# Taking two-head value matmuls apart, and moving two decay steps behind the compressed normalisation, in a two-block fp32 model kernel

## What is computed

```python
for l in range(DEPTH):                       # 2 layers
    proj = rms_norm(x, attn_norm[l]) @ w_in[l]
    ret_o = retention(rope(r_q), rope(r_k), r_v, r_g)      # 6 heads of 64
    nsa_o = nsa(n_q, n_kv, n_g, ...)                       # 6 heads of 64, 2 key/value groups
    gm_o = spatial_gating(gm_z, gm_ws[l], gm_b[l])
    x = x + concatenate([ret_o, nsa_o, gm_o]) @ w_out[l]
    gate, up = split(rms_norm(x, ffn_norm[l]) @ w_gate_up[l])
    x = x + (silu(gate) * up) @ w_down[l]
# nsa, for each head: out = g0 * o_c + g1 * o_s + g2 * o_w
#   o_c: softmax over 15 compressed keys;  o_s, o_w: softmax(q @ k.T + bias) @ v, selected and window branch
# retention, for each head: scores = (q @ k.T) * decay;  o = scores @ v, normalised and gated
```

## Time and profile before

| what | value |
|---|---|
| median of 3 runs | 2002.25 us (2001.49 to 2005.66) |
| the profiled execution: time | 2002.25 us |
| the profiled execution: span of the core | 2000.4 us |
| granted TensorE clock, mean | 0.98 |
| TensorE busy (matmul) | 1882.9 us, 94% |
| VectorE busy | 740.8 us, 37% |
| ScalarE busy | 240.3 us, 12% |
| GpSimd busy | 226.1 us, 11% |

### The profile page before, as it was taken

How to read it: one execution, slowest core, us unless ns; L and a number is a source line. 1 busy time by engine, 2 the same in 40 slices (tenths; PEclk the granted TensorE clock), 3 DMA queues, 4 the chain that set the end, 5 groups by cost and what they waited for, 6 DMA issues and landing times.

```text
span 2000.4 us, 22267 instructions
## 1 busy us (share of the span) xinstructions
PE 1882.9 (94%) x8302; PEld 919.2 (46%) x8302; DVE 740.8 (37%) x1560; ACT 240.3 (12%) x482; POOL 226.1 (11%) x400
## 2 busy tenths in 40 slices
PE   8999999999999999869799999999999999999995
PEld 4466777645577766635433333323332332332331
DVE  3562111155547761794522223222222322322224
ACT  1410000023110000211211101100110110110010
POOL 0200000001018857141000000000000000000000
PEclk9999999999999999979699999999999999999998
DMA  7143433343278845021699999999999999999993
GB/s 300 63 169 133 164 130 126 128 173 121 96 294 319 345 169 218 1 84 53 269 429 429 430 427 429 429 430 426 429 429 430 426 429 429 430 426 429 429 430 164
DMA packets 42766, 583.33 MB, mean 292 GB/s; under 512 B 4726, under 2 KB 5750, under 8 KB 6684
## 3 DMA queue, kind: packets, MB, share of 16 engines
q1 hardware_dynamic: 42236, 581.29, 70.1%
q10 hardware_dynamic: 480, 1.37, 0.2%
HBM read 581.58 MB, written 1.06 MB: 291 GB/s over the span
## 4 chain that ended last, share of the span: by engine, by line
PE 55%; DMA 34%; DVE 9%; ACT 1%; issue 1%; SPq 0%; ACTq 0%; DVEq 0%
DMA ring<-in_exp_w 33%; PE PS L1676 15%; PE PS L1957 10%; PE PS L1404 8%; PE PS L1695 7%; PE PS L1988 3%; PE PS L1581 3%; DVE ring L1107 1%; PE PS L1861 1%; PE PS L1943 1%; PE PS L1918 1%; DMA par<-in_layer_params 1%; PE PS L1451 0%; PE PS L1965 0%; PE PS L1442 0%
## 5 line engine op out<-in xcount | busy, mean ns | idle before, releaser
L1957 PE MATMUL PS<-ring,tb 128*64 128x512 f32 x2176 | 487.2, 598 | 32.6 <-DMA ring<-in_exp_w 31.9
L1957 PEld LDWEIGHTS PS<-ring,tb 128*64 128x64 f32 x2176 | 149.1, 137 | 366.1 <-issue 289.2
L1676 PE MATMUL PS<-hT,ring 128*128 128x256 f32 x1376 | 300.6, 379 | 0.0
L1676 PEld LDWEIGHTS PS<-hT,ring 128*128 128x128 f32 x1376 | 261.1, 190 | 43.0 <-issue 8.6
L1988 PE MATMUL PS<-ring,tb 128*64 128x512 f32 x1088 | 241.0, 595 | 11.5 <-ACT tb L652 11.5
L1404 PE MATMUL PS<-ring,hT 128*128 128x512 f32 (+2 forms) x448 | 187.0, 559 | 2.2 <-ACT hT L407 2.1
L1307 DVE TENSOR_TENSOR hT<-hT,PS 128x512 f32<-128x512 f32 x140 | 96.2, 687 | 233.8 <-PE PS L1943 231.4
L1320 DVE TENSOR_SCALAR tT<-PS 128x512 f32<-128x512 f32 x34 | 23.5, 692 | 425.0 <-PE PS L1965 425.0
L1695 PE MATMUL PS<-ring,tT 128*128 128x512 f32 x352 | 154.7, 593 | 0.0
L1988 PEld LDWEIGHTS PS<-ring,tb 128*64 128x64 f32 x1088 | 77.7, 137 | 152.8 <-issue 152.8
L1035 DVE TENSOR_TENSOR tT<-PS,tT 128x512 f32<-128x512 f32 x22 | 15.2, 692 | 269.6 <-PE PS L1676 269.6
(11 more groups left out here) (426 smaller groups left out, 1612.9 us busy)
## 6 DMA issues: line engine op xcount, KB each, us to landing
ring<-in_exp_w SPq DMA_DIRECT2D x204, 2048.0 KB, 22.8
ring<-in_w_gate_up SPq DMA_DIRECT2D x22, 2048.0 KB, 8.6
ring<-in_ada_w SPq DMA_DIRECT2D x12, 2048.0 KB, 9.2
ring<-in_w_in_part SPq DMA_DIRECT2D x10, 2048.0 KB, 10.2
ring<-in_w_down SPq DMA_DIRECT2D x10, 2048.0 KB, 7.2
ring<-in_w_out SPq DMA_DIRECT2D x6, 2048.0 KB, 8.5
ring<-in_w_in SPq DMA_DIRECT2D x4, 2048.0 KB, 8.2
ring<-in_w_in_part SPq DMA_DIRECT2D x2, 1608.0 KB, 11.6
```

What stands on the lines that cost most here:

```text
L1676: ins = pe.matmul(PS[:, 4 + 2 * (i % 2) + part, 256 * f:256 * f + 256], wt[:, k, 256 * part + 128 * f:256 * part + 128 * f + 128], hT[:, k ...
L1957: ins = pe.matmul(PS[64 * h:64 * h + 64, b, :], xg[:, o:o + 64], ring[:, s, w:w + 512], start=k == 0, stop=False, skip_group_check=True)
```

## The change

Two edits. In the TensorE list, `values` takes one head instead of a pair and is called twice in a step: for head 2p-2 between the second `project(2)` and `turn(2p-1)`, and for head 2p-1 where the pair stood. In the VectorE list, `decayed(2)` and `decayed(3)` move from ahead of the wait for the exponential (`s_c11`) to behind the last step of the compressed softmax.

```diff
@@ VectorE
                 link.to(v.tensor_tensor(pc2, pc2, st[:, 36:48].unsqueeze(2).broadcast_to([P, 12, NCMP]), ALU.subtract), g.s_c10, l + 1)
-                decayed(2)
-                decayed(3)
                 v.wait_ge(g.s_c11, l + 1)
                 link(v.tensor_reduce(st[:, 48:60], pc2, AX_X, ALU.add))
...
                 link.to(v.tensor_tensor(pc2, pc2, st[:, 48:60].unsqueeze(2).broadcast_to([P, 12, NCMP]), ALU.mult), g.s_c12, l + 1)
+                decayed(2)
+                decayed(3)
                 projected(6)
                 decayed(4)
                 decayed(5)
@@ TensorE
-                def values(p):
-                    pe.wait_ge(g.s_pt, l * 12 + 2 * p + 2)
-                    at, vs = [], []
-                    for c in (2 * p, 2 * p + 1):
-                        br, h = c // NH, c % NH
-                        o = (SV, WV)[br] + 64 * (h // 3)
-                        vs.append([proj[:, t, o:o + 64] for t in range(TT)])
-                        at.append((slice(64 * (h % 2), 64 * (h % 2) + 64), 6 + h // 4, 256 * (h // 2 % 2)))
-                    first = p // 3 == 0 and p % 3 in (0, 2)
-                    for i, (rows, bank, o) in enumerate(at):
-                        pe.matmul(PS[rows, bank, o:o + 256], vs[i][0], PT[i][:, 0:256], start=first, stop=False, skip_group_check=True)
-                    for i, (rows, bank, o) in enumerate(at):
-                        pe.matmul(PS[rows, bank, o + 128:o + 256], vs[i][1], PT[i][:, 256:384], start=False, stop=False,
-                                  skip_group_check=True).then_inc(g.s_pv, 1)
+                def values(c):
+                    br, h = c // NH, c % NH
+                    pe.wait_ge(g.s_pt, l * 12 + c + 1)
+                    o = (SV, WV)[br] + 64 * (h // 3)
+                    rows, bank, at = slice(64 * (h % 2), 64 * (h % 2) + 64), 6 + h // 4, 256 * (h // 2 % 2)
+                    pe.matmul(PS[rows, bank, at:at + 256], proj[:, 0, o:o + 64], PT[c % 2][:, 0:256], start=br == 0 and h in (0, 1, 4, 5), stop=False,
+                              skip_group_check=True)
+                    pe.matmul(PS[rows, bank, at + 128:at + 256], proj[:, 1, o:o + 64], PT[c % 2][:, 256:384], start=False, stop=False,
+                              skip_group_check=True).then_inc(g.s_pv, 1)
...
                     project(2)
                     if p >= 1:
+                        values(2 * p - 2)
                         turn(2 * p - 1)
...
                     project(2)
                     if p >= 1:
-                        values(p - 1)
+                        values(2 * p - 1)
```

## The result

The changed kernel takes 2019.41 us (median of 7 runs, 2013.19 to 2020.14), the kernel before, run beside it, 2005.66 us (7 runs, 2001.49 to 2007.66). The ratio is 1.007, with a 95% interval of 1.0059 to 1.0082: slower by 12 to 16 us, 0.7%. Forecast were 12.3 us more, but from a base of 2002.25, and a range up to 2019.0; the time lies 0.4 us outside it. The executions of the kernel before fall into two groups by their mean granted clock: of 64 that ran beside the experiments, 26 took 2000.7 to 2002.6 us at 0.979 or 0.980 and 38 took 2004.7 to 2009.6 us at 0.974 to 0.978, and the profiled one, 2002.25 us at 0.98, belongs to the first.

What follows compares the result with a forecast made beforehand. TensorE's work list in written order was taken to set the time, with delays passed on whole. Value groups 9.6 plus decays 2.7 gave 12.3 us, so 2002.25 + 12.3 = 2014.5 us; range 2009 to 2019 for 8 in 10.

Steps and rivals of the forecast that it cites:

- the sum's base: Whole kernel: the profiled 2002.25 us, also the median of the runs shown, to which 12.3 us were added.
- The decays: Compressed softmax and ret_scores(2): later decays lose 2.12 us, win back 0.78; +1.34 us per layer, +2.7 in all.
- The value groups: Attention steps: each added narrow group pays streaming and edges, 0.78 us in ten steps, 0.89 in two; +9.6 us.
- Rival A: Value groups: edges cost nothing more, 7.5 + 2.7 = 10.2 us, so 2012.4 us; chance 0.80 together with the forecast.
- rival B: Value groups: halves only seem to run together, a single head costs half; 2006.8 us; chance 0.07.
- C: Value groups: a single head can't hide weight loads behind a partner, 9.6 us more; 2024 us; chance 0.05.
- common starts: Paired value matmuls: records start two together, read as both halves running beside each other, a group taking 0.80 us.
- Rival D: Second transposition in the steps: heads fit wholly into a TensorE standstill, decays free; 1995.8 us; chance 0.03.
- The row of the weight loader's idle time: Before the transpositions: 6.5 us idle in 8 cases, put down to VectorE; the most a standstill could hide.
- Rival E: Expert loop: the delay vanishes because expert loads run on and TensorE had slack; 2002.3 us; chance 0.05.
- the second transposition's copy: ScalarE's copy in each step, late by 0.8 us; cover about 1 us, beyond which it is on the path.
- the gating: VectorE work behind the moved decays, wanted by later transposes; ends near 137.8 us, with 1.8 us of cover.

Runs made afterwards that it cites:

- e3: Kernel before, with both heads' value matmuls at the step's end, one head after the other instead of interleaved; 2001.78 us, ratio 0.999.
- e7: Kernel before, with decayed(2) and decayed(3) moved behind projected(6); 2009.35 us, ratio 1.0035.
- e10: Changed kernel with decayed(2) put back in its old place, decayed(3) still moved; 2013.97 us, ratio 1.005.
- e12: Repeat of the kernel before with only decayed(3) moved behind the compressed softmax; one execution, 2007.03 us.
- e9: Kernel of e2 plus 14 unread identity transposes on TensorE ahead of ret_scores(2); 2008.24 us, ratio 1.0021 to the kernel before.
- e11: The changed kernel once more, unaltered; one execution, 2018.74 us.
- e2: Kernel before with only decayed(2) and decayed(3) moved behind the compressed softmax, value matmuls still in pairs; 2013.40 us, ratio 1.0033.
- e1: Changed kernel with both decays back in their old place, so only the value matmuls are taken apart; 2015.69 us, ratio 1.0046.
- e4: Changed kernel with compressed_turn() and a project(4) ahead of ret_scores(2) in TensorE's list; 2014.60 us, ratio 1.0039 to the kernel before.
- e8: Kernel of e1 with the even head's 128-column matmul moved to the step's end, its 256-column one still early; 2008.37 us, ratio 1.0027.

## Why the prediction was wrong, point by point

**The step that failed is the sum's base.** The prediction said: "The profiled execution took 2002.25 us (span 2000.4), which is also the median of the runs". This equality holds for the three runs that were shown. Beside the changed kernel, seven runs gave 2005.66. The traces show where the difference lies. In the last column of the tables the same untouched code takes 1471.1 to 1477.1 us in 14 profiled executions, without order by kernel: the kernel before has 1471.92, e3, whose two layers are equal to it within 0.06 us, 1476.43. Two places carry it in these two. One is the stretch from the first L1718 of the kernel before to its first L1861: 113.59 against 115.88 us. The other lies between the next transposes and the first expert matmul, 32.99 against 35.68. The clock differs in the first: the kernel before, then e3, by stretches of the gated linear attention's part:

```profile
905.00:927.00 22.00, 19.18 (x157) 13.17 (x152) 16.65 (x34) 5.46 (x9) 4.80 (x2) 1.00 0.27 97
```

```profile
906.00:930.00 24.00, 21.66 (x129) 14.18 (x122) 16.57 (x34) 5.33 (x8) 4.72 (x2) 0.79 0.19 78
```

TensorE works there in pieces between waits for VectorE, and the granted clock goes up and down. Together they make 5.0 us; the stretch ahead of them adds 0.4, and the part behind gives 0.8 back. Over all 14 traces the first place takes 113.6 us at a mean granted clock of 0.89 (before, e7, e10, e12), and 115.5 to 115.9 at 0.87 (the other ten). So the spread is there without the change, and the profile before was a light one. Its 2002.25 as base made the forecast 3.4 us too low, and the margin for the spread of the runs, 4.5 us above the likeliest, had to hold this and the next point together. Either alone would have stayed inside the range: 2014.5 + 3.4 = 2017.9, and with one fall of the clock 2014.5 + 1.6 = 2016.1. Of the changed kernel's 18 executions on record three had a mean granted clock of 0.979 or 0.980 and took 2013.2 to 2015.9 us, around the forecast; the other 15, at 0.975 to 0.977, took 2018.7 to 2020.1.

**A term was missing: the clock.** The decays were priced at 2.12 us lost, 0.78 back. Both come out within 0.06 us (2.09, and about 0.72): about 1.37 per layer at full clock (e9, e11, layer 1 of after) for the forecast 1.34. But a fall adds 1.6 us, 1.62 in after and 3.2 for two in e2 against e9. It was in no bound. Before, TensorE never stood still in these stretches for more than 0.7 us at one time, so no row of before showed a fall there; rows of the second block would have: TensorE stands still 9.3 us ahead of L1728, and the granted clock from 865 to 871 us is 0.50.

**The value groups: right, 2% too dear.** Forecast 9.6, measured 9.44 (e1). A group costs the same with one head or two (0.79 and 0.80 us). The single steps of layer 0 are 0.75 (first), 0.76 to 0.77 (second to fourth), 0.72 (fifth) and 0.95 us (sixth) longer; forecast were 0.78 and, for the sixth, 0.89. Part of the fit is luck. In the second step the new group starts 0.53 us after the last wide record, where 0.58 was assumed, and the transposition behind it takes 0.38 us instead of 0.33; the two errors cancel. In the fifth the old stall was 0.30 us and hid more; in the sixth there was none, and the longer transposition shows. Rival A, free edges, would be 7.5 and is out; so are rival B, half the price (e1, and the lone 0.79), and C, exposed weight loads.

**Why a pair is cheap was only half understood.** The prediction read the common starts rightly as two halves running together, but did not say what allows it. Ahead of e3 I expected the alternating list to be needed. It is not: being neighbours is enough.

**Rival D** (the new head fills a standstill): it does swallow the stall that is there, 0.15 us in the second step and 0.2 of 0.3 in the fifth, and no more. The row of the weight loader's idle time overstated it by far, as argued. **Rival E** (the delay vanishes in the expert loop): out; the ratio of after, 14.0 us, is the two layers' 13.8.

**Late behind the moves**: neither the second transposition's copy nor the gating became a wait in the changed kernel. The gating did in e4.

What stays open: why a wait of 2.1 us ends in a fall of the clock in three cases of six. e9 and the lengths of the waits speak for the stillness, but not for what decides a single case. Open too is the second place of the untouched part's spread, 31.5 to 36.3 us: its mean granted clock does not order it (33.0 us at 0.57 in e9, 36.0 at 0.57 in e4). And it is not shown whether the change itself makes the longer executions more frequent (15 of 18, against 38 of 64 before).

## What to carry to other kernels

Price a split of paired narrow matmuls by its groups, not by its instructions: each group between full-width work pays its longer half and its edges again, and the order of the two heads inside made no difference here (e3). When a piece is moved behind a chain, look first at which waiting instruction of the bound engine stands ahead of the one that the move serves; here the transposes were ready sooner and stuck behind scores that came later. And take a base for an absolute forecast from several executions, with a term for the clock wherever a change makes TensorE's longest standstill longer.

## What the runs showed of the hardware that was not expected

The halves of the array overlap over four records of distance: with all four records of one head ahead of the four of the other, the group takes 0.81 us against 0.80 interleaved. The Trainium skill (TensorEngine Tiling (Array Packing), Key Properties) says that different tiles can load and multiply in parallel; e3 agrees, and shows that it holds without interleaving in this case.

A fall of TensorE's clock to its 1.2 GHz level behind a wait costs about three quarters of the wait again: 1.6 us behind one of 2.1. It came in three of six such waits. Filling the wait with 14 useless transposes kept the clock full in both layers and gave 3.2 us back, by the stretches of e9 against e2.

Records of different halves do not start in the order of the list. In the shared group of e8 the second record of the 256-column matmul starts at 69.22 us, after both records of the 128-column matmul that is listed behind it (68.96 and 69.12).
